# A hybrid attention layer on one core: x read once, turned outputs in a bank of their own, values in matmuls of 128 columns

## The reference, cut to what matters

```
h = rmsnorm(x, norm_w)
qa, ka, va, ga, qb, kb, vb, gb = split(h @ w_in)
qa, ka, qb, kb = rope(rmsnorm_per_head(...))             # head width 64
# mixer A: 8 heads, causal, two softmax maps per head
a  = softmax(qa0 ka0') - lam * softmax(qa1 ka1');  oa = a @ va
ya = rmsnorm(oa, subln_w) * (1 - lam_init) * silu(ga)
# mixer B: 16 query heads, 2 key heads, window 128, a sink per head
yb = softmax_with_sink(qb kb') @ vb * silu(gb)
out = x + concat(ya, yb) @ w_out
```

## Time and profile before

| | us |
|---|---|
| median of 3 runs | 2112.53 (2111.04 to 2113.47) |
| the profiled execution, own time | 2114.02 |
| its span in the trace | 2112.3 |
| TensorE busy | 1831.5 (87%) |
| VectorE / ScalarE / GpSimd busy | 1074.9 / 815.0 / 366.1 |
| mean granted TensorE clock | 0.939 of full speed |
| moved by DMA | 244.5 MB |

### The profile page before, as it was taken

One profiled execution on the slowest core, in us unless ns is written; L12 is line 12 of the kernel. 1 busy time (PEld: TensorE's weight loads), 2 busy tenths in 40 slices (PEclk: granted clock), 3 DMA queues, 4 the chain that ended last, 5 costly groups with the idle time before them and its releaser, 6 DMA issues.

```text
span 2112.3 us, 24182 instructions
## 1 busy us (share of the span) xinstructions
PE 1831.5 (87%) x8604; PEld 1541.4 (73%) x8604; DVE 1074.9 (51%) x1779; ACT 815.0 (39%) x1765; POOL 366.1 (17%) x440
## 2 busy tenths in 40 slices
PE   8799898778787888587878787999999996999999
PEld 6599897667676677466667665878888875788887
DVE  2244341364664655545564564577777765332323
ACT  3424231354454454345354443344444433222221
POOL 0000110031331232222221231121111135000000
PEclk9899999888898899789988988999999999999999
DMA  6433234323223323312313233344444458545553
GB/s 227 178 65 99 80 111 129 104 59 114 90 82 95 108 67 108 97 43 86 111 54 119 80 92 109 99 116 116 118 117 122 113 162 297 161 136 150 144 156 114
DMA packets 218360, 244.52 MB, mean 116 GB/s; under 512 B 22528, under 2 KB 141824, under 8 KB 217216
## 3 DMA queue, kind: packets, MB, share of 16 engines
q1 hardware_dynamic: 218240, 242.97, 38.6%
HBM read 182.08 MB, written 60.83 MB: 115 GB/s over the span
## 4 chain that ended last, share of the span: by engine, by line
PE 51%; DVE 13%; DMA 11%; ACT 8%; issue 7%; POOL 5%; SPq 4%; ACTq 0%; POOLq 0%; DVEq 0%
PE ps L854 15%; PE ps L856 15%; PE ps L855 15%; DVE norms_sb L1151 2%; DMA w_raw_sb<-in_wv 2%; DVE w_lo_sb L1058 2%; DMA norms_sb<-in_xT 2%; DVE norms_sb L1058 2%; PE ps L914 2%; DMA tables<-gates_dram 1%; DMA q_dram<-norms_sb 1%; DMA k_dram<-norms_sb 1%; DVE ps L1058 1%; DVE neg_max L1197 1%; PE ps L927 1%
## 5 line engine op out<-in xcount | busy, mean ns | idle before, releaser
L854 PE MATMUL ps<-hT_hi,w_hi_sb 128*128 128x512 f32 x1312 | 555.9, 424 | 46.8 <-DVE w_lo_sb L1058 24.6
L855 PE MATMUL ps<-hT_lo,w_hi_sb 128*128 128x512 f32 x1312 | 536.5, 409 | 0.0
L856 PE MATMUL ps<-hT_hi,w_lo_sb 128*128 128x512 f32 x1312 | 535.2, 408 | 0.0
L1058 DVE TENSOR_TENSOR w_lo_sb<-w_raw_sb,w_hi_sb 128x512 fp32r<-128x512 f32 (+1 forms) x340 | 262.7, 773 | 500.8 <-ACT w_hi_sb L618 498.2
L618 ACT ACTIVATE w_hi_sb<-w_raw_sb 128x512 fp32r<-128x512 f32 (+1 forms) x340 | 207.9, 612 | 510.8 <-PE ps L856 277.4
L854 PE MATMUL ps<-w_hi_sb,hT_hi 128*128 128x512 f32 (+1 forms) x896 | 335.5, 374 | 40.6 <-DVE w_lo_sb L1058 40.4
L854 PEld LDWEIGHTS ps<-hT_hi,w_hi_sb 128*128 128x128 f32 x1312 | 264.6, 202 | 106.4 <-DVE w_lo_sb L1058 33.2
L855 PE MATMUL ps<-w_lo_sb,hT_hi 128*128 128x512 f32 (+1 forms) x896 | 332.9, 372 | 0.0
L856 PE MATMUL ps<-w_hi_sb,hT_lo 128*128 128x512 f32 (+1 forms) x896 | 332.5, 371 | 0.0
L856 PEld LDWEIGHTS ps<-hT_hi,w_lo_sb 128*128 128x128 f32 x1312 | 261.7, 199 | 60.7
L855 PEld LDWEIGHTS ps<-hT_lo,w_hi_sb 128*128 128x128 f32 x1312 | 263.4, 201 | 51.6
(11 more groups left out here) (148 smaller groups left out, 2251.9 us busy)
## 6 DMA issues: line engine op xcount, KB each, us to landing
w_raw_sb<-in_wp SPq DMA_DIRECT2D x148, 256.0 KB, 3.3
w_raw_sb<-in_w_out SPq DMA_DIRECT2D x128, 256.0 KB, 3.2
q_dram<-norms_sb SPq DMA_DIRECT2D x64, 256.0 KB
attention_sb<-q_dram SPq DMA_DIRECT2D x128, 128.0 KB, 3.1
w_raw_sb<-in_wv SPq DMA_DIRECT2D x48, 192.0 KB, 2.3
norms_sb<-in_xT SPq DMA_DIRECT2D x16, 512.0 KB, 6.1
exp_sb<-in_x SPq DMA_DIRECT2D x8, 1024.0 KB, 6.3
attention_sb<-v_dram SPq DMA_DIRECT2D x64, 128.0 KB, 3.4
```

The source lines that it names most:

```text
L854: pe.matmul(dst, a_hi, b_hi, start=start, stop=False)
L855: pe.matmul(dst, a_hi, b_lo, start=False, stop=False)
L856: return pe.matmul(dst, a_lo, b_hi, start=False, stop=stop)
L1058: return dve.tensor_tensor(o, a, b, op)
```

## The change

- **Start.** x is no longer read row by row. ScalarE squares each xT tile as it lands, GpSimd adds the 16 squares up, and four matmuls against a matrix of 1/2048 give the mean for every token. One round trip of the row factor through DRAM goes.
- **Slots of the A steps.** Transposes of the probabilities and values come one slot later (`tp = s1 + 3`; narrow `pv = tp + 2`). Narrow steps use the two halves of the probability buffers by turns.
- **Outputs.** `turn_o` writes to `B_SS`, the bank of the sums of squares. ScalarE reads it (`y_out`). Each of the two users of that bank waits until the other's last use has been read (`ss_bank_free`).
- **Values.** `three()` with 128 columns per matmul; `second` copies the sum out, and `join` for mixer A goes.
- **Tables.** One `preload_act_table_set` of a set with Ln and Exp.
- **GpSimd** takes the lo subtracts of the jobs (`job_lo`), and from slot 238 multiplies A's outputs by their gates, which are stored as `y_gated_dram`; `load_prep` then reads one tensor for them instead of two.
- **SyncE** issues the weight load first in each slot, two units ahead instead of three; several stores come one to two slots later.

```diff
-B_PROJ, B_TR, B_O, B_SS = [2, 6], [3, 7], 4, 5
+B_PROJ, B_TR, B_O, B_SS = [3, 7], [4, 5], 2, 6
...
-            self.tp = self.s1 + 2
-            self.pv = self.tp + (2 if wide else 1)
+            self.tp = self.s1 + 3
+            self.pv = self.tp + 2
...
+    SS_USES += [("O", _st.g) for _st in steps_at("to", _hs)] + [("ss", _j) for _j in jobs_at("ss", _hs)]
...
             for slot in range(-48, NHS):
-                u = U_V + slot + 48 if slot < 0 else U_T + slot // 2
-                if slot < 0 or slot % 2 == 0:
-                    load_w(u + 3)
+                if slot < 0:
+                    load_w(sp, U_V + slot + 48 + 2)
+                elif slot % 2 == 0:
+                    load_w(sp, U_T + slot // 2 + 2)
...
             def load_prep(j):
+                if k < AH:
+                    for c in range(2):
+                        sp.wait_ge(yg_stored[c], 16 * AH)
+                    sp.dma_start(dst, scr_z[k, :, t]).then_inc(y_in[j % 8], 16)
+                    return
...
+                    act.preload_act_table_set("natural_log_exp_and_others")
...
+            def y_out(st):
+                act.wait_ge(to_done, st.g + 1)
+                wait(act, y_stored[st.g % 3], 16 * (st.g // 3))
+                act.activation(y_of(st), ps[:, B_SS, 0:P], ACT.Copy, scale=pars[:, C_SUB:C_SUB + 1]).then_inc(y_ready, 1)
...
+            def ss_bank_free(use):
+                n = SS_USES.index(use)
+                if n:
+                    what, m = SS_USES[n - 1]
+                    pe.wait_ge(y_ready if what == "O" else u_ready, m + 1)
...
             def sum_squares(j):
-                wait(pe, u_ready, j if j >= 4 else 0)
+                if j >= 4:
+                    ss_bank_free(("ss", j))
...
-                        pe.matmul(p_o[:, 0:2 * P], aT_hi[:, a], v, start=b == 0, stop=False)
-                        mm = pe.matmul(p_o[:, 0:P], aT_lo[:, a], v[:, 0:P], start=False, stop=b == st.i)
+                        mm = three(p_o[:, 0:P], aT_hi[:, a], aT_lo[:, a], v[:, 0:P], v[:, P:2 * P], b == 0, b == st.i)
...
             def turn_o(st):
-                n = USE["O", st.g]
                 pe.wait_ge(o_ready, st.g + 1)
-                wait(pe, tp_free, n - 1)
-                pe.transpose(ps[:, B_TR[n % 2], 0:P], o_of(st), ident[:, :]).then_inc(tp_done, 1)
+                ss_bank_free(("O", st.g))
+                pe.transpose(ps[:, B_SS, 0:P], o_of(st), ident[:, :]).then_inc(to_done, 1)
...
+            for half, evacuated in enumerate((p0_act, p0_dve)):
+                pe.matmul(ps[:, 4 * half, :], ones, x_acc_hi[:, t], start=True, stop=False)
+                pe.matmul(ps[:, 4 * half, :], ones, x_acc_lo[:, t], start=False, stop=True).then_inc(acc_sum, 1)
...
+            def job_lo(j):
+                pool.wait_ge(hi1, j + 1)
+                pool.tensor_tensor(r(bufY[d]), bufY[d], B, ALU.subtract).then_inc(lo1, 1)
```

More of the change, by code:

```diff
@@ L118, in __init__ @@
             self.after = x + 3
+        self.narrow = not wide
+        self.base = (g % 2) * 512 if self.narrow else 0
+        self.alone = self.narrow and self.i > 0
         w = (self.i + 1) * P
@@ L253, in o_of, with y_of, y_count @@
             return o_sb[:, (st.g % 2) * P:(st.g % 2 + 1) * P]
-        o_part = o_sb[:, 2 * P:3 * P]
+        def y_of(st):
+            return y_st[:, (st.g % 3) * P:(st.g % 3 + 1) * P]
+        def y_count(n, slot):
+            return (n + 2 - slot) // 3
         def v_block(st, b):
@@ L314, in prep_hk, with b_item, gate_item @@
             return j // KT, j % KT
+        def b_item(j):
+            half, k = prep_hk(j)
+            return half * AH + k - AH
+        def gate_item(slot):
+            n, c = divmod(slot - GATED_FROM, GATED_EVERY)
+            return n if c == 0 and 0 <= n < 2 * AH else None
         def prep_items(slot):
@@ L452, in store_y @@
                 if st.a:
-                    sp.wait_ge(tp_free, USE["O", st.g] + 1)
-                    sp.dma_start(scr_y[st.unit, :, t], y_st[:, (st.g % 2) * P:(st.g % 2 + 1) * P])\
-                        .then_inc(y_stored[st.g % 2], 16)
+                    sp.wait_ge(y_ready, st.g + 1)
+                    sp.dma_start(scr_y[st.unit, :, t], y_of(st)).then_inc(y_stored[st.g % 3], 16)
                     return
@@ L530, in _ @@
                     store_job(j)
-                if slot == -7:
+                if slot == -5:
                     for m in range(3):
@@ L823, in _ @@
                         exp_a(st, 1)
+                for st in steps_at("to", slot):
+                    y_out(st)
                 for st in steps_at("sq", slot):
@@ L904, in turn_probs @@
                     pe.wait_ge(comb_done, st.g + 1)
-                    blocks = [expd[:, 1, b * P:(b + 1) * P] for b in range(st.i + 1)]
+                    blocks = [expd[:, 1, st.base + b * P:st.base + (b + 1) * P] for b in range(st.i + 1)]
                 else:
@@ L1045, in _ @@
                         pe.wait_ge(tp_free, len(USE))
+                        pe.wait_ge(y_ready, AH * NR)
                         pe.wait_ge(o_read, NS)
@@ L1322, in _ @@
             split_w(U_V + 1)
+            dve.wait_ge(acc_hi, 1)
+            tt(x_acc_lo, x_acc, f(x_acc_hi), ALU.subtract).then_inc(acc_lo, 1)
             for b in range(4):
@@ L1329, in _ @@
             dve.wait_ge(pars_ready, 3)
+            for half in range(2):
+                dve.wait_ge(acc_sum, half + 1)
+                dve.tensor_scalar(row_b[:, half * 512:(half + 1) * 512], ps[:, 4 * half, :], EPS, None, ALU.add)\
+                   .then_inc(rows_ready, 1)
+            dve.wait_ge(ident_ready, 2)
+            dve.wait_ge(rows_ready, 2)
+            diag = sin_t.rearrange("p (r t) -> p r t", r=NR)
+            tt(diag, row_b[:, :].rearrange("p (r t) -> p r t", r=NR),
+               ident[:, :].unsqueeze(1).to_broadcast([P, NR, P]), ALU.mult).then_inc(rows_ready, 1)
+            dve.wait_ge(rows_ready, 3)
+            dve.tensor_reduce(ss_x[:, 0, :], diag, AX, ALU.add).then_inc(rows_ready, 1)
             for slot in range(-48, NHS + 1):
@@ L1362, in _ @@
                 for st in steps_at("pv", slot):
-                    join(st)
-                for st in steps_at("to", slot):
-                    y_out(st)
+                    if not st.a:
+                        join_b(st)
                 for st in steps_at("s1", slot):
@@ L1384, in _ @@
                         job_prod2(j)
-                for j in jobs_at("out", slot):
-                    job_lo(j)
                 if slot < NHS:
@@ L1426, in x_rms @@
             def x_rms():
[L1427 to L1435 removed]
+                for k in range(1, KT):
+                    pool.wait_ge(x_sq, k + 1)
+                    wait(pool, x_added, k - 1)
+                    pool.tensor_tensor(x_acc, x_acc, x_sq_sb[k % 2], ALU.add).then_inc(x_added, 1)
+                pool.wait_ge(rows_ready, 4)
+                pool.tensor_tensor(ss_x[:, 2, :], ss_x[:, 0, :], small[:, 0, :], ALU.pow).then_inc(rms_chain, 1)
             def job_add(j):
@@ L1496, in _ @@
                         job_o2(j)
+                for j in jobs_at("out", slot):
+                    job_lo(j)
+                n = gate_item(slot - 1)
+                if n is not None:
+                    multiply_gates(n)
                 for j in prep_items(slot):
-                    prep_mul(j)
+                    if prep_hk(j)[1] >= AH:
+                        prep_mul(j)
 def tile_columns():
```

355 lines of the change are left out of this document (194 added, 161 removed).

## The result

The changed kernel takes 2160.42 us (median of 4, 2152.45 to 2162.49); the kernel before takes 2112.86 us on the same chip. The ratio is 1.022, 95% interval 1.0193 to 1.0246: **slower by 47.6 us, where 1983 us, 129 us faster, was forecast.** The profiled execution is the fastest of the four, 2152.45 us with a span of 2150.7.

A forecast was written before the change was run, and what follows sets the result against it. TensorE was taken as the bound, idle behind late VectorE and ScalarE. Start -18, values -15, attention -83 (-151 +51 -16 +33), its begin +2, output units -15: -129, from 2112.3 to 1983 us; own range 1950 to 2020.

The forecast's parts named there:

- Start: First stage, 121.5 us: reads of x and row squares go, idle time and half the clock loss saved; -18 us.
- The lead of the weight loads: Value loads get one unit less lead; the attention stage's begin gets +2 us for the fourth unit's load behind value stores.
- Values' stage: Stage of 234.3 us: later stores free SyncE, half the idle time and half the clock loss saved; -15 us.
- The new wait: Attention stage: sum of squares waits for ScalarE's read of the turned output in 13 slots; +51 us.
- Rival 1: The wait of the sum of squares is hidden because ScalarE reads the turned tile early; 1894 us, chance 0.19.
- The turned output's bank: Attention stage: with own bank, later values and fewer table loads, 151 of 196.3 us idle go; -151 us.
- Values in three matmuls: Attention stage: matmul count sets the pace, 288 blocks at 0.115 us more each; +33 us.
- Clock: Attention stage: 22 long stalls instead of 27, each costing 2.9 us at the lower clock; -16 us.
- Mixer B: Mixer B's stage: TensorE's slots cover the gating's added multiplies and DMA; 0 us, bound +5.
- Output units: Change to the output units, 77.1 us: half the tiles need one load instead of two; -15 us, bounds 0 and -25.
- Rival 2: TensorE meets late engines at values and scores instead, half of the old waits come back; 2055 us, chance 0.16.
- rival 4: GpSimd's slower lo subtracts delay freeing ScalarE's buffer, so TensorE waits for a bank; 2133 us, chance 0.04.

The follow-up runs named there:

- e1: Changed kernel with each weight load issued three units ahead, as before the change: 2072.06 us, 0.9780 of the kernel before.
- b2: Kernel before with only the weight loads issued two units ahead instead of three: 2276.46 us, 1.0765 of the kernel before.
- e2: Changed kernel with ScalarE's read of the turned output moved ahead of the exponentials of its slot: 2104.69 us, 0.9938 of the kernel before.
- e11: e7 with the turned output back in the two banks of the turned probabilities: 2018.99 us, 0.9525 of the kernel before.
- e7: e6 with mixer A's values as before the change (two matmuls a block, join on VectorE): 2010.78 us, 0.9505 of the kernel before.
- b3: Kernel before with only the one preload of a table set for Ln and Exp: 2085.55 us, 0.9848 of the kernel before.
- e12: e7 without the one preload of a table set: 2064.83 us, 0.9737 of the kernel before.
- e10: e7 with transposes of the probabilities and values back in their earlier slots: 2023.12 us, 0.9550 of the kernel before.
- b1: Kernel before with only mixer A's values as three matmuls, sum copied out by ScalarE, no join: 2120.04 us, 1.0021 of the kernel before.
- e6: Changed kernel with weight loads three units ahead and the turned output read ahead of the exponentials: 2020.95 us, 0.9550 of the kernel before.
- e4: Changed kernel with the jobs' lo subtracts back on VectorE: 2151.69 us, 1.0158 of the kernel before.
- e8: e7 with the jobs' lo subtracts back on VectorE: 2014.85 us, 0.9514 of the kernel before.

## Why the prediction was wrong

The forecast was -129 from 2112 and ended on the wrong side, which had been given a chance of 0.04. By its own steps, each with the difference of the stages:

- **Start: right.** -18 forecast, bounds to -24; -23.1 measured. The clock is 1.00 in the stage instead of 0.93, all of its loss came back.
- **The lead of the weight loads: the step that failed first.** The diff's `u + 3` to `u + 2` was priced in two places, as half of an unknown in the values and as "+2" at the begin of the attention stage. The attention stage proper and mixer B's stage got no term for it and no reason for leaving it out. It costs 93 us here (e1) and 162 by itself in the kernel before (b2). What was missed: the load and its split now stand in the same slot, SyncE comes to its slots late, a third of the loads take over 5 us and up to 13.4 to land, and on ScalarE and VectorE the exponentials and maxima of the slot are queued behind the split. For the sum of squares the prediction named what is queued behind the waiting instruction; for the split it did not.
- **Values' stage: wrong sign.** -15 forecast, +3.2 measured, -7 with three units ahead (e1): it was the same cause.
- **The new wait: right in place, number and mechanism, short in size.** 13 stalls, 51 us forecast, 64.8 measured. Rival 1 (hidden) is out. Moving one line takes the 60 us away (e2), so most of it was the price of the order in ScalarE's list and not of the shared bank; 12.9 us of the wait stay.
- **The turned output's bank: the second step that failed.** "-151" counted the 76 us of stalls at L949 as a gain of the bank. With the bank shared again (e11) 45 us of such stalls come back and the stage is 1.4 us longer. There the stalls were where the lateness of ScalarE and VectorE showed, not what made TensorE late. Of the -151, the repaired kernel e7 keeps 42 (idle 154.2 after 196.3), or 56 if the 14.1 us left of the new wait are counted apart, as the forecast did.
- **Table loads: right thing, underrated.** They were one argument among several inside the -151; alone they are 32 us before (b3) and 49 in the repaired kernel (e12). They are the largest part of what e7 gains in this stage, 62 us.
- **Later slots for transposes and values:** forecast to cover most of L927's 27.7 us; worth 10 us in the repaired kernel (e10).
- **Values in three matmuls: right in busy time, wrong in time.** +33 forecast; the block takes 0.33 us as said, busy time grew by 25 in the stage (b1), and the kernel by 4 us, or 10 the other way round (e7). In this stage, with 196 us of idle time, the added work was not paid for in full.
- **Clock: -16 forecast,** 0.89 measured, no change. It follows the stalls: 0.91 in e2, 0.93 in e6.
- **Mixer B: 0 forecast,** bound +5; +12.4 measured. The prediction had named new idle time in this stage as the sign that would break the forecast. The gating is not its cause: with it in place and the loads three units ahead the stage is 5 us shorter than before (e1).
- **Output units: -15 forecast,** -5.6 measured, within the bounds.

Rival 2 (lateness finds the next wait) described what TensorE's rows look like, 57.7 us at L962 with the unnamed ones, but it expected old lateness to move. What came was new lateness. No rival held the loads, and the slower side was left to rival 4, whose mechanism is worth 13 us with late loads (e4) and nothing measurable without (e8). One sum is off, with nothing resting on it: the four stretches named as idle (196.3, 24.6, 21.8, 24.6) add up to 267 us, and the 277 takes in mixer B's 9.6, a stage whose clock is 1.00.

Open: why the shorter lead costs more in the kernel before than in the changed one, how much of the 93 us a shorter landing would have saved, and what the 13 us of e4 are.

## What to carry to other kernels

When engines walk one list each, ask for every transfer in which slot it is issued, in which slot its first reader stands, and what the reader has queued behind it, and read its longest landing and not the median. One unit of lead was worth 4.4% and 7.65% here. A large row in the waits of the bottleneck names the place where lateness is paid, and freeing that place can gain little while the engine behind it is late, as in e11: shorten that engine's list (table loads) or put first what others wait for. Price work added to an engine with idle time by an experiment, not by its sum.

## What the runs showed of the hardware that was not expected

Nothing that the engines do differently than in the trace of before. The weight loads took about as long: median 3.4 us from issue to landing after the change, 3.3 before. Not expected was how far the longest lie from the median: of 98 equal loads of 256 KB, 31 took over 5 us after the change (up to 13.4), 26 before (up to 10.8), 31 in e1 (up to 13.5). In the 9.56 us of the load shown above the DMA engines moved 234 GB/s, against 87 in the mean of the stage; that the company of other transfers made it slow is likely and was not tried. Two sizes were not expected either: 51 table loads of 1.283 us, 65 us of ScalarE's time on an engine that is busy for 39% of the span, cost the kernel 32 to 49 us; and the weight loads' lead moved mixer B's stage, with TensorE busy for 97% of it, by 69 us.
